# Break of the stick: in three of four heads VectorE adds up the later blocks' softplus tiles

## The reference

```
scale = d ** -0.5
z = einsum('bhtd,bhsd->bhts', q, k) * scale
causal = kpos < qpos                                  # strictly
log_1m_beta = where(causal, -softplus(z), 0)
rev_incl = cumsum(log_1m_beta, axis=3, reverse=True)
rev_excl = rev_incl shifted left by one, 0 at the end
a = where(causal, exp(log_sigmoid(z) + rev_excl), 0)
out = einsum('bhts,bhsd->bhtd', a, v)
```

## Time and profile before

| | |
|---|---|
| time, median of 3 runs | 2421.44 us (2421.01 to 2422.19) |
| profiled execution | 2421.1 us, its span 2419.4 us |
| TensorE busy | 2372.0 us (98%), 11994 products |
| VectorE busy | 1012.5 us (42%) |
| ScalarE busy | 904.9 us (37%) |
| GpSimd busy | 1125.2 us (47%) |
| mean granted TensorE clock | 0.986 |

### The profile page before, as it was taken

One profiled execution on the slowest core, in us unless ns is written; L12 is line 12 of the kernel. 1 busy time (PEld: TensorE's weight loads), 2 busy tenths in 40 slices (PEclk: granted clock), 3 DMA queues, 4 the chain that ended last, 5 costly groups with the idle time before them and its releaser, 6 DMA issues.

```text
span 2419.4 us, 29753 instructions
## 1 busy us (share of the span) xinstructions
PE 2372.0 (98%) x11994; PEld 1985.2 (82%) x11994; DVE 1012.5 (42%) x1513; ACT 904.9 (37%) x1037; POOL 1125.2 (47%) x1486
## 2 busy tenths in 40 slices
PE   6999999999999999999999999999999999999998
PEld 5888888888887878888878888888888787888886
DVE  6676566624442341221356666440444423221223
ACT  3223233256667332332333222233556843332332
POOL 2444544543434545554644454444434345554552
PEclk7999999999999999999999999999999999999999
DMA  7443535322212323323243544223122123223231
GB/s 236 161 156 120 166 123 163 122 70 70 66 57 70 105 79 95 105 87 105 87 140 124 173 132 134 92 70 105 54 69 70 53 88 95 96 87 105 92 100 53
DMA packets 244152, 252.46 MB, mean 104 GB/s; under 512 B 4016, under 2 KB 241728, under 8 KB 244032
## 3 DMA queue, kind: packets, MB, share of 16 engines
q1 hardware_dynamic: 242496, 247.53, 31.8%
q10 hardware_dynamic: 1536, 3.17, 0.4%
HBM read 248.59 MB, written 2.10 MB: 104 GB/s over the span
## 4 chain that ended last, share of the span: by engine, by line
PE 96%; DVE 1%; ACT 1%; DMA 1%; issue 0%; SPq 0%; DVEq 0%; ACTq 0%
PE proj L701 65%; PE proj L738 11%; PE proj L723 7%; PE att L843 4%; PE att L795 2%; PE att L828 1%; PE att L777 1%; PE att L855 1%; PE proj L668 1%; PE att L687 1%; DVE slab L966 1%; PE att L804 1%; DMA work<-in_w_ada 0%; DMA ya<-in_x 0%; PE att L660 0%
## 5 line engine op out<-in xcount | busy, mean ns | idle before, releaser
L366 POOL TENSOR_TENSOR w_lo<-w_raw,w_hi 128x256 fp32r<-128x256 f32 x1472 | 1123.0, 794 | 1257.6 <-ACT w_hi L405 1256.6
L405 ACT ACTIVATE w_hi<-w_raw 128x1024 fp32r<-128x1024 f32 x368 | 385.1, 1054 | 560.5 <-PE proj L701 473.6
L701 PE MATMUL proj<-h_hi,w_hi 128*128 128x512 f32 x1504 | 591.3, 393 | 0.0
L701 PE MATMUL proj<-h_lo,w_hi 128*128 128x512 f32 x1504 | 587.3, 390 | 0.0
L701 PE MATMUL proj<-h_hi,w_lo 128*128 128x512 f32 x1504 | 586.8, 390 | 0.0
L701 PEld LDWEIGHTS proj<-h_hi,w_lo 128*128 128x128 f32 x1504 | 283.2, 188 | 59.8
L701 PEld LDWEIGHTS proj<-h_hi,w_hi 128*128 128x128 f32 x1504 | 283.1, 188 | 58.9 <-issue 0.3
L701 PEld LDWEIGHTS proj<-h_lo,w_hi 128*128 128x128 f32 x1504 | 283.3, 188 | 57.3
L701 PE MATMUL proj<-y_lo,w_hi 128*128 128x512 f32 x832 | 323.8, 389 | 0.0
L701 PE MATMUL proj<-y_hi,w_lo 128*128 128x512 f32 x832 | 323.8, 389 | 0.0
L701 PE MATMUL proj<-y_hi,w_hi 128*128 128x512 f32 x832 | 323.8, 389 | 0.0
(11 more groups left out here) (153 smaller groups left out, 2522.3 us busy)
## 6 DMA issues: line engine op xcount, KB each, us to landing
w_raw<-in_w_in SPq DMA_DIRECT2D x88, 1024.0 KB, 5.1
slab<-in_w_ada SPq DMA_DIRECT2D x40, 1024.0 KB, 7.7
w_raw<-in_w_up SPq DMA_DIRECT2D x32, 1024.0 KB, 5.5
w_raw<-in_w_down SPq DMA_DIRECT2D x32, 1024.0 KB, 5.0
w_raw<-in_w_ret_out SPq DMA_DIRECT2D x16, 1024.0 KB, 5.0
work<-in_w_ada SPq DMA_DIRECT2D x8, 1024.0 KB, 5.5
w_raw<-in_w_sb_out SPq DMA_DIRECT2D x8, 1024.0 KB, 5.0
w_raw<-in_w_mix_out SPq DMA_DIRECT2D x8, 1024.0 KB, 5.0
```

The costliest lines, as they stand in the source:

```text
L366: ins = pool.tensor_tensor(w_lo[:, s, ks, :], w_raw[:, s // 2, ks, P * (s % 2):P * (s % 2 + 1)], w_hi[:, s, ks, :], ALU.subtract)
L405: act.activation(w_hi[:, 2 * s + j, :, :], w_raw[:, s, :, P * j:P * (j + 1)], ACT.Copy).then_inc(hi_ready, 1)
L701: last = pe.matmul(proj[:, j, :], w[:, slot, k, :], a[:, k, :], start=k == 0 and n == 0, stop=k == KT - 1 and n == 2)
```

## The change

In three of four heads (all but head 1 of the even pairs) VectorE adds up the later blocks' softplus tiles, and TensorE multiplies the sums. In terms, block 3's tile is added to block 2's columns from 128 on, then block 2's to block 1's columns from 128 on. The sums for blocks 0 and 1 (384 and 256 columns) are split into a high and a low part, written over terms' own space as later; for block 2 the later sum is block 3's own tile, which exists. That is six VectorE instructions a head, five of them linked to the next. In the break these heads take 6 all-ones products, widths 384, 256 and 128 twice each, instead of 12. The products are also put in another order: the triangular products of both heads first, then head 0's all-ones products, then head 1's. TensorE waits for later_ready before a summed head's all-ones products, and ScalarE before it writes the weights over terms.

```
+def is_summed(n, a):
+    return n % 2 == 1 or a == 0
...
+        later_hi = (later[:, :, 0:384], later[:, :, 768:1024], sp_hi[:, :, OFF[3]:OFF[3] + P])
+        later_lo = (later[:, :, 384:768], later[:, :, 1024:1280], sp_lo[:, :, OFF[3]:OFF[3] + P])
...
                     for a in range(2):
                         act.wait_ge(broken, 2 * n + a + 1)
                         act.wait_ge(sp_ready, 2 * n + a + 1)
+                        if is_summed(n, a):
+                            act.wait_ge(later_ready, sums_later(n, a))
                         act.activation(terms[:, a, :], scores_of(a), ACT.Exp).then_inc(weights_exp, 1)
...
                     for a in range(2):
                         pe.wait_ge(sp_ready, 2 * n + a + 1)
                         for i in range(TB):
-                            for j in range(i, TB):
-                                at = 3 * a * SEQ + OFF[i] + P * (j - i)
-                                for sp_part in (sp_hi, sp_lo):
-                                    last = pe.matmul(att_flat[:, at:at + WID[j]],
-                                                     (neg_tri if i == j else neg_ones)[:, :],
-                                                     sp_part[:, a, OFF[j]:OFF[j] + WID[j]],
-                                                     start=False, stop=True, skip_group_check=True)
+                            for sp_part in (sp_hi, sp_lo):
+                                add_product(a, OFF[i], neg_tri, sp_part[:, a, OFF[i]:OFF[i] + WID[i]])
+                    for a in range(2):
+                        if is_summed(n, a):
+                            pe.wait_ge(later_ready, sums_later(n, a))
+                        for i in range(TB - 1):
+                            for part_of, sp_part in ((later_hi, sp_hi), (later_lo, sp_lo)):
+                                if is_summed(n, a):
+                                    last = add_product(a, OFF[i] + P, neg_ones, part_of[i][:, a, :])
+                                else:
+                                    for j in range(i + 1, TB):
+                                        last = add_product(a, OFF[i] + P * (j - i), neg_ones,
+                                                           sp_part[:, a, OFF[j]:OFF[j] + WID[j]])
                         last.then_inc(broken, 1)
...
+                def sum_later(n):
+                    for a in range(2):
+                        if not is_summed(n, a):
+                            continue
+                        dve.wait_ge(sp_ready, 2 * n + a + 1)
+                        t0, t1, t2, t3 = (terms[:, a, OFF[j]:OFF[j] + WID[j]] for j in range(TB))
+                        own.link(dve.tensor_tensor(t2[:, P:], t2[:, P:], t3, ALU.add))
+                        own.link(dve.tensor_tensor(t1[:, P:], t1[:, P:], t2, ALU.add))
+                        for i, t in enumerate((t1, t2)):
+                            own.link(dve.tensor_copy(later_hi[i][:, a, :], t))
+                            ins = dve.tensor_tensor(later_lo[i][:, a, :], t, later_hi[i][:, a, :], ALU.subtract)
+                            if i == 0:
+                                own.link(ins)
+                        ins.then_inc(later_ready, 1)
...
                     softplus(n)
                     for half in range(2):
+                        if half == 1:
+                            sum_later(n)
                         taken(pair, at, half)
                         dve.tensor_tensor(ya[:, ds(2 * g + half, 1), :], ya[:, ds(2 * g + half, 1), :],
                                           gate_t.rearrange("p (a n) -> p a n", a=1), ALU.mult).then_inc(gate_used, 1)
                     mask_weights(n)
                     low_output(n, ds(2 * g, 1))
                     softplus(n + 1)
+                    sum_later(n + 1)
                     mask_weights(n + 1)
```

More of the change, by code:

```diff
@@ L69, with sums_later @@
 CAUSAL = sum(WID)
+TERMS_AT = 6144
+def is_summed(n, a):
+    return n % 2 == 1 or a == 0
+def sums_later(n, a):
+    return 3 * (n // 2) + (1 if n % 2 == 0 else 2 + a)
 V_AT, P_AT = 2048, 6144
@@ L127, in hybrid_trunk @@
         p_lo = nc.alloc_sbuf_tensor_at("p_lo", [P, CAUSAL], f32r, offset=work_base + 4 * P_AT)
+        later = nc.alloc_sbuf_tensor_at("later", [P, 2, CAUSAL], f32r, offset=work_base + 4 * TERMS_AT)
         ident = sb("ident", [P, P])
@@ L176, in hybrid_trunk @@
         sb_now = part(3072, 3, 1024)
-        terms = part(6144, 2, CAUSAL)
+        terms = part(TERMS_AT, 2, CAUSAL)
+        later_hi = (later[:, :, 0:384], later[:, :, 768:1024], sp_hi[:, :, OFF[3]:OFF[3] + P])
+        later_lo = (later[:, :, 384:768], later[:, :, 1024:1280], sp_lo[:, :, OFF[3]:OFF[3] + P])
         gate_t = part(8704, SEQ)
@@ L239, in hybrid_trunk @@
         sb_done, sb_half, sb_ready = sem("sb_done"), sem("sb_half"), sem("sb_ready")
-        qk_now, v_now = sem("qk_now"), sem("v_now")
+        qk_now, v_now, later_ready = sem("qk_now"), sem("v_now"), sem("later_ready")
         gate_used, merged_sum, merged_half, merged_ready = (
@@ L835, in break_stick, with add_product @@
                 def break_stick(n):
+                    def add_product(a, at, weights, softplus_part):
+                        return pe.matmul(att_flat[:, 3 * a * SEQ + at:3 * a * SEQ + at + softplus_part.shape[-1]],
+                                         weights[:, :], softplus_part, start=False, stop=True, skip_group_check=True)
                     for a in range(2):
```

## The result

The changed kernel takes 2435.02 us (median of 4, 2434.35 to 2435.71) against 2421.34 us, ratio 1.0055 with the interval 1.004 to 1.007. It is slower by 13.7 us; the forecast was 2434, with 2418 to 2443 around it.

The account below looks back on a forecast made before the run. TensorE was taken to bound the kernel, with 96% of the span. Even pairs -5.5, odd pairs +11.4 and clock +6.8 gave +12.7 us on 2421.1 us: 2434 us, with 8-in-10 range 2418 to 2443.

Parts of the forecast that it names:

- The price of a sum: VectorE's six linked instructions per summed head, alternating with GpSimd, cost 5.06 us a head against 2.5 us free.
- The wait: TensorE waits for second-head sums in odd pairs: 2.63 us in six, 3.35 us in each layer's last group.
- one link in a hole between GpSimd's sets: Last groups' odd pairs: 0.4 us taken off VectorE's two-head chain, ending it at 762.2 instead of 762.6.
- Sum of the odd pairs: Longer breaks in eight odd pairs: 6 x 1.25 + 2 x 1.95 = 11.4 us lost.
- The gain: Fewer all-ones products in the break save TensorE 0.69 us a summed head, 16.6 us over 24 heads without waits.
- the 0.3 us of slack: Even pairs: head 0's sums ready at 529.8, needed at 530.15, so TensorE doesn't wait, by 0.3 us.
- The clock: Eight new TensorE waits may drop its clock, 1.7 us a fall, 0 to 13.6 us; half taken, 6.8 us.
- The faster one: Rival, chance 0.13: VectorE's sums run at free price or GpSimd gets out of the way, nothing waits, 2404.5 us.
- The one without falls: Rival, chance 0.16: the same alternation of VectorE and GpSimd, but TensorE's clock doesn't fall, 2427 us.
- The two conditions that separated the cases: Whether sums take under 0.6 us per VectorE instruction in odd pairs, and whether TensorE's clock falls at the waits.
- the sum: Whole kernel: -5.5 (even pairs) + 11.4 (odd pairs) + 6.8 (clock) = +12.7 us, giving 2434 us.
- its three terms: Even pairs -5.5 us, odd pairs +11.4 us, TensorE clock falls +6.8 us.

Follow-up runs that it names:

- The ten discarded products: Changed kernel plus ten 512-column products, results thrown away, in front of TensorE's wait in odd pairs: 2426.33 us, ratio 1.0021.
- the moved half unit: Changed kernel, but in odd pairs the following half unit's first 12 of 24 products stand between head 0's and head 1's all-ones products: 2405.55 us.
- the products alone: Changed kernel without sums and waits for them; the six all-ones products read the blocks' own softplus tiles: 2405.5 us, ratio 0.9935.

## Why the prediction was right

**The price of a sum.** It was read from the chain of the earlier trace rows and not from the free prices, and this decided the sign. After: 0.98, 0.78, 0.98, 0.71, 0.84 us for the first head, 0.82, 0.85, 0.78, 0.96, 0.70, 0.83 for the second, with gaps 5.1 us a head against 5.06. The casts, for which rows gave 0.83 and 0.49 us at 512 columns, came out at 0.78 and 0.70, the side that was taken. With memsets in place of GpSimd's reads the additions and subtractions were back at their free prices, beside memsets too, so for them the cause is shown. For the casts it is shown less sharply, since memsets held some of them up as well.

**The wait.** Predicted 2.63 us and a break 1.25 us longer in six odd pairs. Measured: idle for 2.44 us, the next products begun 2.6 us later than the 0.11 us behind the last ones that they take without a wait, and breaks 1.3 us longer. In the last groups 3.35 and 1.95 were predicted; idle for 2.67, 2.8 later and 1.52 longer were measured. There I allowed for one link in a hole between GpSimd's sets; the timeline after, VectorE and then GpSimd, shows two at their free price:

```profile
765.19 0.36 DVE L1207 CAST later<-work 128x384 fp32r<-128x384 f32 x1
765.59 0.56 DVE L1208 TENSOR_TENSOR later<-work,later 128x384 fp32r<-128x384 f32 x1
...
765.84 3.50 POOL L382 TENSOR_TENSOR w_lo<-w_raw,w_hi 128x256 fp32r<-128x256 f32 x4 [0.96 <-ACT w_hi L421]
```

Sum of the odd pairs: 11.4 predicted, 10.9 measured.

**The gain.** 0.69 us a head, exactly. Even pairs wait for nothing, as the 0.3 us of slack said, though the trace shows how near it was: the sums of the first pair end at 530.66 + 0.84 = 531.50, 0.3 us before their first product at 531.80, and in the other seven even pairs it is 0.30 to 0.35 us.

**The clock.** Half of the waits were charged with a fall, 6.8 us; four of eight fell, 6.4 us. That it was four was luck, since rows could only bound it; that a fall costs 1.7 us (1.5 to 1.6 measured over a half unit) and that idling causes it was right. The ten discarded products show it, and in none of the other kernels, where TensorE waits for no sum or for 1.0 us at most, does the clock fall in the stick-breaking parts.

**The rivals.** The faster one (2404.5) needed sums under 0.6 us an instruction; it is what happens when GpSimd doesn't read (all breaks short), and what the moved half unit reaches by another way (2405.5). The one without falls (2427) is the kernel with discarded products (2426.3); with the waits left idle it did not come true, since idle times of 2.44 us were enough for a fall in four of them. The two conditions that separated the cases were thus the right ones.

**What was too simple.** I charged all clock falls to the new waits. Falls in unchanged stretches come and go between profiles too, and the one at 475.9 moved the profile after by 1.6 us; what brings them is open. The forecast owes part of its closeness to that: the sum said +12.7 us, its three terms measured -5.5 + 10.9 + 6.4 = +11.8, and the rest of the measured difference lies where the sum had nothing.

## What to carry to other kernels

A chain of short VectorE instructions beside a GpSimd that reads SBUF costs about 0.85 us a link here (5.1 us for six, two casts among them), where the free prices are 0.3 to 0.55 us; price it by such a chain in the trace, and ask how many links fit before the bounding engine needs the end. Where they didn't fit, moving twelve independent products (half of a half unit) into the wait recovered all that the products alone give, clock included. Moving work from the bounding engine to an idle one pays as far as the idle engine's answer is in time, and of the three heads of a group that were moved, two were in time.

## What the runs showed of the hardware

Memsets on GpSimd left VectorE's additions and subtractions at their free price but held up a cast: 1.05 us instead of 0.36 for 384 columns. It began at 553.47, while memsets started every 0.15 us, so it was kept back over several of them and not over one; it ended at 554.52, 0.21 us after the last of that set of eight. Casts of 0.76 us (at 616.50) and 1.47 us (at 745.59) stand in the same trace. The Trainium skill, page "SBUF — State Buffer", section "Who interferes with whom", has the first half (two-input instructions contend only with GpSimd's reads, casts in a two-port mode with any); that the cast waits through several instructions is not what its rule of one whole instruction lets expect.

The length of the wait alone does not decide whether the clock falls: behind idle times of 2.44 us it fell four times in six, behind the two of 2.67 us in the last groups it did not.
